# Second mixer of a hybrid decoder step: low score levels as compact 32x32 blocks in one batch per tile, TensorE's tile loops written out, gate rows loaded behind a weight chunk

## What is computed

```python
def step(s, inp):                     # _gla_core, per chunk
    qc, kc, vc, ac = inp
    b = jnp.cumsum(ac, axis=1)
    decay = jnp.exp(jnp.where(mask, b[:, :, None] - b[:, None], -jnp.inf))
    att = jnp.einsum('bthk,bshk,btshk->bhts', qc, kc, decay)
    o = jnp.einsum('bhts,bshv->bthv', att, vc) + jnp.einsum('bthk,bhkv->bthv', qc * jnp.exp(b), s)
    bl = b[:, -1]
    s = s * jnp.exp(bl)[..., None] + jnp.einsum('bshk,bshv->bhkv', kc * jnp.exp(bl[:, None] - b), vc)
    return s, o
```

```python
z = h @ p['w_in']
zh, zr, zg, zm, zgate = _split(z, IN_SIZES)
...
proj = jnp.einsum('btnc,ncd->btnd', outs, p['w_branch'])
gates = jax.nn.sigmoid(zgate).reshape(B, T, N_BRANCH, D_MODEL)
mix = jnp.sum(proj * gates, axis=2) @ p['w_out']
```

## Time and profile before

| | |
|---|---|
| three runs | 2133.0, 2136.48 and 2138.94 us, median 2136.48 |
| profiled execution | 2138.09 us, of which the span of the trace is 2136.5 |
| busy share of the span | PE 97%, PEld 92%, DVE 49%, ACT 28%, POOL 21% |
| mean granted clock of TensorE | 0.983 |
| second mixer's 8 tiles | about 395 to 695 us |
| third mixer's 8 tiles | about 849 to 1090 us |

### The profile page before, as it was taken

The page is one execution under the profiler, slowest core; times in us unless marked ns, Lnnn a source line. Parts: engine busy times, 40 slices in busy tenths (PEclk is TensorE's granted clock), DMA queues, the critical chain, the costliest instruction groups (busy, mean ns, idle before and its releaser), DMA issues.

```text
span 2136.5 us, 37031 instructions
## 1 busy us (share of the span) xinstructions
PE 2067.6 (97%) x15223; PEld 1959.4 (92%) x15223; DVE 1038.5 (49%) x1629; ACT 605.1 (28%) x825; POOL 443.1 (21%) x463
## 2 busy tenths in 40 slices
PE   7999999999999989999899999999999999999997
PEld 5999888999999868888789999999999999999996
DVE  6143334365665545444344786522222245656566
ACT  4332224332322254222222431110100123333343
POOL 1223113344463511100002771200000010000020
PEclk9999999999999989999998999999999999999999
DMA  4122226222221332011114751311111252111112
GB/s 181 41 60 78 79 83 175 62 69 65 68 68 60 123 124 81 27 48 43 42 42 164 253 201 50 121 49 39 49 43 65 90 195 77 39 49 40 49 40 102
DMA packets 50995, 177.95 MB, mean 83 GB/s; under 512 B 6496, under 2 KB 10176, under 8 KB 50640
## 3 DMA queue, kind: packets, MB, share of 16 engines
q1 hardware_dynamic: 25440, 85.77, 13.6%
q0 software_dynamic: 17648, 61.31, 8.6%
q10 hardware_dynamic: 7808, 29.41, 3.6%
HBM read 128.95 MB, written 47.51 MB: 83 GB/s over the span
## 4 chain that ended last, share of the span: by engine, by line
PE 85%; DVE 8%; DMA 3%; issue 2%; ACT 2%; DVEq 0%; POOL 0%; SPq 0%; ACTq 0%
PE PS L481 29%; PE PS L677 22%; PE PS L1628 16%; PE PS L1600 2%; PE PS L1235 2%; DMA RING<-in_w_all 1%; DVE AR L2673 1%; PE PS L1247 1%; DMA RING<-in_w_br 1%; PE PS L1270 1%; DVE OT_parts L655 1%; PE PS L1263 1%; DVE CF_parts L651 1%; PE PS L1316 1%; PE PS L1406 1%
## 5 line engine op out<-in xcount | busy, mean ns | idle before, releaser
L481 PE MATMUL PS<-HT_parts,WHIA_parts 128*128 128x352 f32 (+1 forms) x1440 | 513.6, 357 | 14.9 <-POOL RING_parts L476 5.8
L481 PE MATMUL PS<-OT_parts,WHIA_parts 128*128 128x352 f32 (+1 forms) x1440 | 475.6, 330 | 0.0
L481 PE MATMUL PS<-HT_parts,RING_parts 128*128 128x352 f32 (+1 forms) x1440 | 474.7, 330 | 0.0
L481 PEld LDWEIGHTS PS<-HT_parts,WHIA_parts 128*128 128x128 f32 x1440 | 278.2, 193 | 31.3 <-issue 12.6
L476 POOL TENSOR_TENSOR RING_parts<-RING,WHIA_parts 128x1024 fp32r<-128x1024 f32 x58 | 150.7, 2599 | 695.7 <-ACT WHIA_parts L471 695.7
L481 PEld LDWEIGHTS PS<-OT_parts,WHIA_parts 128*128 128x128 f32 x1440 | 278.7, 194 | 2.9 <-issue 0.3
L481 PEld LDWEIGHTS PS<-HT_parts,RING_parts 128*128 128x128 f32 x1440 | 277.6, 193 | 0.0
L1628 PE MATMUL PS<-MIXHI_parts,CF_parts 128*128 128x352 f32 x786 | 253.8, 327 | 5.0 <-DVEq L2923 2.9
L677 PE MATMUL PS<-HT_parts,CF_parts 128*128 128x352 f32 x768 | 249.4, 325 | 0.9 <-ACT AR L644 0.9
L677 PE MATMUL PS<-HT_parts,RING_parts 128*128 128x352 f32 x768 | 249.5, 325 | 0.0
L677 PE MATMUL PS<-OT_parts,CF_parts 128*128 128x352 f32 x768 | 249.2, 325 | 0.0
(11 more groups left out here) (463 smaller groups left out, 3348.2 us busy)
## 6 DMA issues: line engine op xcount, KB each, us to landing
RING<-in_w_all SPq DMA_DIRECT2D x132, 512.0 KB, 3.7
AR<-gates POOLq DMA_DIRECT2D x32, 528.0 KB, 4.0
proj<-AR ACTq DMA_DIRECT2D x18, 537.0 KB, 5.2
AR<-proj POOLq DMA_DIRECT2D x18, 537.0 KB, 7.4
gates<-CF ACTq DMA_DIRECT2D x16, 528.0 KB, 5.3
gates<-AR ACTq DMA_DIRECT2D x16, 528.0 KB, 5.5
AR<-in_xT SPq DMA_DIRECT2D x8, 537.0 KB, 8.8
AR<-in_xT POOLq DMA_DIRECT2D x8, 528.0 KB, 6.0
```

The costliest lines, as they stand in the source:

```text
L481: last = e.matmul(out, a_[:, u, k, :], b_[:, k, t], start=first and i == 0, stop=end and i == 2)
```

## The change

1. **Scores.** In the 8 full tiles the levels with half sizes 1 to 16 and the diagonal no longer go through `GQC`, `GQB` and full-width multiplications. They lie inside the 32x32 blocks on the diagonal of the tile. PE multiplies for each of 6 slots, head and block of 32 tokens: 64 or 32 rows by 32 by 16 columns (32 in the diagonal's slot). That is 192 small multiplications in one batch, after 8 filling steps. ACT copies the batch from four banks into `GSC` (6 copies). DVE selects in a compact `GATC` (6 selects), copies the four blocks into `GATT`, and does levels 32 and 64 as before. The 48 filling steps are placed as 8, 4, 4, 16, 2, 8 and 6. POOL spreads only two levels by head. The last tile is as before.
2. **Loops.** PE's tile loops of the second and third mixer are written out (`for` in place of `e.Fori`), so that each tile has its own instructions. The other engines keep theirs.
3. **Gate rows.** The four loads into `OTG` are issued after POOL's `weight_lo` for chunk 0 of filling 8, in place of before (two ahead of the state outputs, two after filling 7's second row was written).

The core of the diff:

```diff
-            for i, slot in ((4, 0), (5, 1)):
-                e.dma_start(OTG[:, slot], proj_row(i)).then_inc(S("rows2"), 16)
...
-            for i, slot in ((8, 2), (9, 3)):
-                e.dma_start(OTG[:, slot], proj_row(i)).then_inc(S("rows2"), 16)
...
             weight_lo(e, 0, P_FILL + Q_RW + 1)
+            for i, slot in ((4, 0), (5, 1), (8, 2), (9, 3)):
+                e.dma_start(OTG[:, slot], proj_row(i)).then_inc(S("rows2"), 16)
...
+                def by_blocks():
+                    e.wait_ge(S("gl_qk"), n * 7 + 5)
+                    e.wait_ge(S("gl_dk"), n + 1)
+                    e.sem_inc(S("select_turn"), 1)
+
+                    for sl in range(6):
+                        for g in range(2):
+                            for b in range(4):
+                                blk = slice(32 * b, 32 * b + 32)
+                                for j in range(2):
+                                    r = slice(64 * j, 64 * j + 64)
+                                    if sl < 5:
+                                        k_ = x[r, g, sl + 1, blk]
+                                        e.matmul(PS(1 + j, sl * 32 + g * 16, sl * 32 + g * 16 + 16)[blk], k_, half(k_, HALVES[sl], True),
+                                                 start=True, stop=True)
...
+                    for sl in range(6):
+                        for b in range(4):
+                            blk = slice(32 * b, 32 * b + 32)
+                            for i, bank in enumerate((1, 4, 2, 5)):
+                                r = slice(32 * i, 32 * i + 32)
...
+                    last.then_inc(S("gl_s"), 1)
+                    steps(gate, 4)
+                    for l in (6, 7):
...
+                        steps(gate, 4 if l == 6 else 16)
...
-                with e.Fori(first, end) as n:
+                for n in range(first, end):
                     gl_tile(n, P, False, fill_work(e, n + Q_GL_TILES, first > 0))
...
-            with e.Fori(1, TILES // 2) as i:
+            for i in range(1, TILES // 2):
...
+                    steps(outs, 1)
+                    e.wait_ge(S("gl_s"), n * 3 + 1)
+                    for j in range(2):
+                        e.activation(GSC[:, :, j:4:2, :], PS(1 + j, 0, 224).rearrange("p (s g c) -> p s g c", s=7, g=2), ACT.Copy)
...
+            def gl_block_selects(n):
+                e.wait_ge(S("gl_sc"), n + 1)
```

More of the change, by code:

```diff
@@ L1222, in gl_tile, with by_levels @@
                 steps(gate, 16 if last_tile else 8)
-                for l in range(1, nl + 1):
-                    if l >= 3:
-                        e.wait_ge(S("gl_att"), n * 8 + l - 2)
-                    if l == 2:
-                        e.wait_ge(S("gl_v"), n + 1)
-                    if l < nl:
-                        e.wait_ge(S("gl_qb"), n * 7 + l)
-                        m = w // 2
+                def by_levels():
+                    a0, q0 = TILES, TILES * 2
+                    for l in range(1, nl + 1):
+                        if l >= 3:
+                            e.wait_ge(S("gl_att"), a0 + l - 2)
+                        if l == 2:
+                            e.wait_ge(S("gl_v"), n + 1)
+                        if l < nl:
+                            e.wait_ge(S("gl_qb"), q0 + l)
+                            m = w // 2
+                            for g in range(3):
+                                lo, hi = ((0, 2), (2, 4), (4, 8))[g]
+                                last = e.matmul(PS(3 * (l % 2), lo * m, hi * m)[0:w], x[:, g, l, 0:w],
+                                                GQB[:, l % 2, lo * m:hi * m], start=True, stop=True)
+                        else:
+                            e.wait_ge(S("gl_dk"), n + 1)
+                            for h in (5, 0, 2, 4, 1, 3, 6, 7):
+                                r, g = ((slice(64 * (h % 2), 64 * (h % 2) + 64), h // 2) if h < 4
+                                        else (slice(32 * (h - 4), 32 * (h - 4) + 32), 2))
+                                if h == 7:
+                                    e.wait_ge(S("gl_sc"), n + 1)
+                                b, c = GL_DIAG[h]
+                                last = e.matmul(PS(3 * (l % 2) + b, c * w, c * w + w)[0:w], x[r, g, nl + 1, 0:w],
+                                                q[r, g, 1, 0:w], start=True, stop=True)
+                                if h == 5:
+                                    last.then_inc(S("gl_sc"), 1)
+                        last.then_inc(S("gl_s"), 1)
+                        steps(gate, 2)
@@ L1251, in gl_tile @@
-                    last.then_inc(S("gl_s"), 1)
-                    steps(gate, 2 if last_tile else 3)
+                            last = e.matmul(PS(3 * (l % 2), lo * 64, hi * 64), x[:, g, l, :], GQB[:, l % 2, lo * 64:hi * 64],
+                                            start=True, stop=True)
+                        last.then_inc(S("gl_s"), 1)
+                        steps(gate, 4 if l == 6 else 16)
+                if last_tile:
+                    by_levels()
+                else:
+                    by_blocks()
@@ L2498, in gl_tile @@
             def gl_tile(n, ahead):
-                gl_selects(n, False)
+                gl_block_selects(n)
                 if ahead:
```

132 lines of the change are left out of this document (87 added, 45 removed).

## The result

The changed kernel takes 2191.7 us in the median of its executions (2162.1 to 2201.6), the kernel before 2136.6. The ratio is 1.020 with a 95% interval from 1.015 to 1.025; executed again beside other kernels it was 1.026 (1.022 to 1.030, median 2192.7, 2180.0 to 2209.3). The range of the prediction ended at 2172. The forecast had the right sign. It was far off in one term, the clock in the second mixer, and had no such term for the third.

The account below looks back on a forecast made before the run. PE was taken as the bound, busy 97% of the span. Scores -27.4, instruction supply +40, clock +4, third mixer's loops -5.2, gate rows 0: +11.4 us, 2147.9 for the median, range 2104 to 2172.

Parts of the forecast that it names:

- the right sign: Whole kernel: forecast slower, +11.4 us, to 2147.9 us for the median of the runs.
- the clock in the second mixer: Second mixer's batches: half clock behind two stops of 2.5 us costs 4 us more over eight tiles, bounds 0 and 20.

Follow-up runs that it names:

- first looped profile: Profile of the changed kernel with the second mixer's tiles as a loop again on TensorE, the rest of the change kept; median 2111.6 us, ratio 0.988.

## What to carry to other kernels

Count the instructions of a dense group against the rate at which blocks of code arrive before writing a loop out; either keep the group in a loop whose body stays in the instruction memory (here 1174 instructions did and 1942 didn't), or put work between pieces of half a block, so that a block lasts the 4 us that the next one takes. Price a stop of TensorE not by its length alone but with the clock behind it, above all where it falls between small matmuls, and look at several executions' mean clocks before trusting one profile. When a kernel's time spreads by more than its neighbours', look where the 256-instruction borders fall: some additional instructions in the right place can be worth more than an optimization.

## What the runs showed of the hardware

- TensorE's granted clock was at full or at half and nowhere between, in all sixteen profiles; half clock came in stretches of 3.41 to 23.89 us. Behind a stop of about 1 us one of 17.07 us made a tile 37.6 us long in place of 29.0.
- Small multiplications back to back, 384 records in 3.5 us, left it at 1.00 in all six later rounds of the first looped profile. Small groups between single filling steps brought it down in two tiles with no wait above 0.5 us ahead.
- The changed kernel's batches came 40.8 to 41.1 us apart from tile 2 on, though they meet the borders in different places: in its first profile the stretch of half clock began 40.96 us behind the one before, seven times.
- A loop body of 1174 instructions was fetched once (0 packets of q8 over four tiles), one of 1942 in every round (10 packets a tile).
- 60 instructions with 0.25 us of work (an estimate from 8.4 ns a record) changed the median by 12 us and the spread of the executions from 32 to 50 us; 160 of them changed the changed kernel's median by 32 us.
